# Attention by couples of query rows, with six banks of scores, one bank of turned probabilities and scores five chunks ahead

## The reference, cut to what matters

```
def mla_block_attend(qn, qp, kn, kp, v, qpos, kpos):
    s = jnp.einsum('bqhd,bkhd->bhqk', qn, kn) + jnp.einsum('bqhr,bkr->bhqk', qp, kp)
    s = jnp.where(chunk_mask(qpos, kpos), s.astype(F32) * MLA_SCALE, NEG_INF)
    p = jax.nn.softmax(s, axis=-1).astype(v.dtype)
    return jnp.einsum('bhqk,bkhd->bqhd', p, v)
```

## Time and profile before

| | us |
|---|---|
| median of 3 runs | 3041.34 (3039.64 to 3042.31) |
| the profiled execution | 3039.4 |
| its span, first to last instruction | 3037.6 |
| attention, first S of turn 1 to the end of turn 4 | 1396 to 2058 |
| one turn of chunks (the second), first S to first K of the next | 1566.49 to 1718.61 |

### The profile page before, as it was taken

The page is one execution under the profiler, slowest core; times in us unless marked ns, Lnnn a source line. Parts: engine busy times, 40 slices in busy tenths (PEclk is TensorE's granted clock), DMA queues, the critical chain, the costliest instruction groups (busy, mean ns, idle before and its releaser), DMA issues. The chain is left out here.

```text
span 3037.6 us, 69418 instructions
## 1 busy us (share of the span) xinstructions
PE 2722.8 (90%) x28140; PEld 2005.5 (66%) x28140; DVE 1761.0 (58%) x3745; ACT 1090.9 (36%) x2589; POOL 551.4 (18%) x516
## 2 busy tenths in 40 slices
PE   6999999999999999957989999898998399999970
PEld 6988888888888888844555555554554255555540
DVE  1566666666666666655767586772322644444428
ACT  1233333333333333324545454551222033333336
POOL 0000000000000000001000000001111356566635
PEclk9999999999999999969999999999999699999995
DMA  6222222122221212232010101004554399999537
GB/s 202 40 39 39 39 38 41 37 41 38 40 38 38 38 37 41 41 80 91 1 41 1 41 1 38 1 1 157 156 160 145 152 318 338 370 325 297 135 71 242
DMA packets 336907, 303.11 MB, mean 100 GB/s; under 512 B 236655, under 2 KB 291983, under 8 KB 322193
## 3 DMA queue, kind: packets, MB, share of 16 engines
q1 hardware_dynamic: 318016, 248.31, 26.9%
q0 software_dynamic: 18576, 50.36, 7.1%
HBM read 208.64 MB, written 85.47 MB: 97 GB/s over the span
## 5 line engine op out<-in xcount | busy, mean ns | idle before, releaser
L801 PE MATMUL mx_bank<-mx_xT,mx_w_in 128*128 128x128 f32 x5168 | 646.0, 281 | 18.5 <-DVEq L264 13.7
L801 PEld LDWEIGHTS mx_bank<-mx_xT,mx_w_in 128*128 128x128 f32 x5168 | 600.5, 193 | 62.1 <-issue 37.5
L1502 PE MATMUL at_bank<-pl_kT,pl_qT 128*128 128x512 f32 (+5 forms) x656 | 288.4, 526 | 2.3 <-issue 2.3
L2245 POOL DMA_INDIRECT ex_x<-scr_hx,ex_plan x192 | 239.2, 1246 | 65.2 <-issue 57.9
L1464 ACT ACTIVATE at_PQ<-at_bank,at_nms 128x512 f32<-128x512 f32 (+5 forms) x328 | 193.6, 596 | 118.6 <-DVE at_nms L1603 115.6
L697 ACT ACTIVATE mx_pr<-mx_bank 128x256 f32<-128x256 f32 (+1 forms) x68 | 36.6, 540 | 554.6 <-PE mx_bank L801 471.9
L1534 PEld LDWEIGHTS at_bank<-at_PT,at_vals 128*64 128x64 f32 (+1 forms) x2208 | 117.4, 136 | 146.0 <-issue 81.1
L1599 DVE TENSOR_REDUCE at_mx<-at_bank 128x1 f32<-128x512 f32 (+5 forms) x328 | 188.8, 576 | 43.0 <-PE at_bank L1502 38.5
L652 POOL TENSOR_TENSOR mx_AR<-mx_u,mx_ep 128x512 f32<-128x512 f32 x17 | 20.1, 1181 | 1001.3 <-DVE mx_kh L1141 1001.3
L1514 PE MATMUL at_bank<-pl_at_ident,at_PQ 128*128 128x128 f32 x1104 | 183.6, 281 | 15.9 <-ACT at_PQ L1464 9.8
L1514 PEld LDWEIGHTS at_bank<-pl_at_ident,at_PQ 128*128 128x128 f32 x1104 | 125.7, 140 | 99.3 <-issue 47.7
(11 more groups left out here) (348 smaller groups left out, 5379.3 us busy)
## 6 DMA issues: line engine op xcount, KB each, us to landing
pl_wg<-in_w_eg SPq DMA_DIRECT2D x32, 1024.0 KB, 8.8
pl_wu<-in_w_eu SPq DMA_DIRECT2D x32, 1024.0 KB, 13.0
pl_wd<-in_w_ed SPq DMA_DIRECT2D x32, 1024.0 KB, 9.1
mx_x<-in_x SPq DMA_DIRECT2D x76, 128.0 KB, 3.8
scr_acc<-ro_blank SPq DMA_DIRECT2D x19, 512.0 KB, 6.3
pl_ro_x<-in_x SPq DMA_DIRECT2D x17, 512.0 KB, 5.4
scr_hx<-ro_h SPq DMA_DIRECT2D x17, 512.0 KB, 2.7
scr_acc<-ro_ha SPq DMA_DIRECT2D x17, 512.0 KB, 3.2
```

The costliest lines, as they stand in the source:

```text
L801: ins = pe.matmul(dst, w_in[:, k, col:col + n], xT[:, k, :], start=(k == 0), stop=(k == KC - 1))
L1502: t.mark(pe.matmul(bank[n % SB][:, 0:wd], qT[h][keys(h), j * P:(j + 1) * P], kT[h][keys(h), k0 * P:k0 * P + wd], start=True, stop=True), f ...
L2245: x_in[s].go(g.indirect_dma_start(x[s][:, k, :], None, rows, bass.IndirectOffsetOnAxis(ap=idx[:, at:at + 1], axis=0)))
```

## The change

The rows are taken in couples (0,1), (2,3) to (14,15), and 16 alone. PV of a couple takes one key block for both rows at once where both see it (256 columns), and for the higher row alone where only that one does (128 columns). PT is laid out in 16 slots that hold a chunk of each row of the couple, side by side. The units of a couple start only when the higher row's head 1 chunks are turned, and are given to every second step, two key blocks at a time, or four a step for the couple before the last row. Bank 7 holds 256 columns of sums and 256 of reciprocals, and recT, its copy and out are done once for a couple. AHEAD becomes 5, SB 6 and TB 1. A turn then has 33 steps with units, 74 key blocks (64 of them for two rows, so 138 units as before) and 9 row ends.

```diff
-    AHEAD, SB, TB = 4, 5, 2
+    AHEAD, SB, TB = 5, 6, 1
     LAG = 3
-    NP, NPT = 4, 14
+    NP, NS = 4, 16
...
+    couples = [(j, j + 1) for j in range(0, NT - 1, 2)] + [(NT - 1,)]
...
+    step = 0
+    for q, js in enumerate(couples):
+        mine = [(g, s) for p, g, s in pairs if p == q]
+        following = 2 * len(couples[q + 1]) * len(groups(couples[q + 1][-1])) if q < last_couple else 0
+        stride = 2 if following >= 4 else 1
+        burst = max(2, -(-len(mine) // max(1, following // 2))) if stride == 2 else 4
+        step = max(step, place[js[-1], 1, 0] + LAG)
+        for at in range(0, len(mine), burst):
+            part = mine[at:at + burst]
+            step = max(step, place[js[-1], 1, part[-1][0]] + LAG)
+            share[step] = len(part)
+            last_step = step
+            step += stride
+        row_end[last_step] = q
+        step = max(step, last_step + 2)
...
+                            for h in range(2):
+                                hs = slice(64 * h, 64 * h + 64)
+                                slot = slot_of[place[high, h, gi]] % NS
+                                left = vals[0:rows, k0 + s, hs]
+                                if both:
+                                    ins = pe.matmul(bank[7][hs, 0:2 * P].rearrange("p (a n) -> p a n", a=2), left,
+                                                    PT[0:rows, slot, :, s, :], start=first, stop=end)
...
+                for r in range(len(couples[q])):
+                    ins = pe.transpose(bank[7][:, (2 + r) * P:(3 + r) * P],
+                                       wide[:, q % 2, r].rearrange("p a n -> p (a n)"), ident[:, :])
+                t.mark(ins, f"recT{q}")
...
+                t.mark(v.tensor_tensor(o_sb[:, js[0]:js[-1] + 1, :], bank[7][:, 0:wd].rearrange("p (a n) -> p a n", n=P),
+                                       recb[:, 0:wd].rearrange("p (a n) -> p a n", n=P), ALU.mult), f"out_{j}")
```

More of the change, by code:

```diff
@@ L1279, in ends @@
         return n == count - 1 or chunks[n + 1][:2] != chunks[n][:2]
-    pairs = [(j, g, s) for j in range(NT) for g in range(len(groups(j))) for s in range(groups(j)[g][1])]
-    share, row_end = {}, {}
[L1284 to L1292, removed]
+    couples = [(j, j + 1) for j in range(0, NT - 1, 2)] + [(NT - 1,)]
+    couple_of = {j: q for q, js in enumerate(couples) for j in js}
+    last_couple = len(couples) - 1
+    turned = [(q, h, g) for q, js in enumerate(couples) for h in range(2) for g in range(len(groups(js[-1])))]
+    slot_of = {}
+    for m, (q, h, g) in enumerate(turned):
+        for j in couples[q]:
+            slot_of[place[j, h, g]] = m
+    freed_by = {n: turned[m - NS] for n, m in slot_of.items() if m >= NS and chunks[n][0] == couples[turned[m][0]][0]}
+    pairs = [(q, g, s) for q, js in enumerate(couples) for g in range(len(groups(js[-1]))) for s in range(groups(js[-1])[g][1])]
+    share, row_end = {}, {}
+    step = 0
[13 more added lines that the diff above has]
+        step = max(step, last_step + 2)
     steps = max(max(share) + 1, count)
@@ L1311, in pv_names @@
         out = []
-        for j, g, s in pairs[first:first + share.get(n, 0)]:
-            if s == groups(j)[g][1] - 1:
-                out.append(f"PV{j}_{g}")
+        for q, g, s in pairs[first:first + share.get(n, 0)]:
+            if s == groups(couples[q][-1])[g][1] - 1:
+                out.append(f"PV{q}_{g}")
         return out + ([f"recT{row_end[n]}"] if n in row_end else [])
@@ L1531, in values, with row_rec @@
                             rows = last if s == k - 1 else P
+                            first = gi == 0 and s == 0
+                            both = len(js) == 2 and k0 + s <= low
                             end = gi == len(gs) - 1 and s == k - 1
-                            for h, m in ((0, m0), (1, m1)):
-                                ins = pe.matmul(bank[7][64 * h:64 * h + 64, 0:P], vals[0:rows, k0 + s, 64 * h:64 * h + 64],
-                                                PT[0:rows, m % NPT, s, :], start=(gi == 0 and s == 0), stop=end)
+                            for h in range(2):
[5 more added lines that the diff above has]
+                                                    PT[0:rows, slot, :, s, :], start=first, stop=end)
+                                else:
+                                    c = P * (len(js) - 1)
+                                    ins = pe.matmul(bank[7][hs, c:c + P], left, PT[0:rows, slot, high % 2, s, :],
+                                                    start=first, stop=end)
                             if s == k - 1:
-                                t.mark(ins, f"PV{j}_{gi}")
+                                t.mark(ins, f"PV{q}_{gi}")
                             yield
-            def row_rec(t, j):
-                t.w(vec, f"rec_wide{j}_1")
-                t.mark(pe.transpose(bank[7][:, P:2 * P], wide[:].rearrange("p a n -> p (a n)"), ident[:, :]), f"recT{j}")
+            def row_rec(t, q):
+                t.w(vec, f"rec_wide{couples[q][-1]}_1")
+                for r in range(len(couples[q])):
+                    ins = pe.transpose(bank[7][:, (2 + r) * P:(3 + r) * P],
+                                       wide[:, q % 2, r].rearrange("p a n -> p (a n)"), ident[:, :])
+                t.mark(ins, f"recT{q}")
             def turn(t):
@@ L1639, in turn @@
                         t.w(ten, f"PT{n}")
-                        if n >= NPT:
-                            j, _, g = chunks[n - NPT]
-                            t.w(ten, f"PV{j}_{g}")
+                        if n in freed_by:
+                            q, _, g = freed_by[n]
+                            t.w(ten, f"PV{q}_{g}")
                         wd, _ = width(n)
```

55 lines of the change are left out of this document (31 added, 24 removed).

## The result

The changed kernel takes 3070.76 us in the median of 4 runs (3067.07 to 3072.73), the kernel before 3041.82 in the runs beside it. The ratio is 1.0097, with a 95% interval of 1.0085 to 1.0110: slower by about 29 us, where +14 was forecast. The profiled execution took 3070.69 us, its span is 3068.8, against 3039.4 and 3037.6.

The account below looks back on a forecast made before the run. PE was taken as the bound, 137.4 of 152.1 us a turn. First steps +0.1, middle -0.4 and tail +3.8 made +3.5 a turn, +14 in four, so 3055 us, range 3047 to 3062 (0.43).

Parts of the forecast that it names:

- +1.9 and -2.3: Middle of a turn: steps 24 to 47 become 1.9 us longer, steps 48 to 75 become 2.3 us shorter.
- 256 columns do run side by side: Units of couples: the rival said they don't, so units double, 29 us a turn, 3170; chance 0.02.
- products cost by number: Bursts: rival that half of the 0.33 us goes with product count, 3.5 us a turn, 3041; extreme 3011; chance 0.05.
- The 60 cycles for each matmul: PE's passes, 1184 for 2208: the skill's overhead rule would gain 26 us more than the sum, 3029.
- the sum for a turn: Whole turn: +0.1 first steps, -0.4 middle, +3.8 tail, together +3.5 us, +14 in four turns.
- the clock is no part of this: PE in turn 2 of the kernel before: granted clock of 1.00, so no term for the clock.
- Steps 0 to 23: Start of a turn: one more max, 0.3 us less of outs, bank waits about as large as old waits; +0.1 us.
- Tail, +3.8: From T75 to the next turn: 16.7 us for 12.9, of which 3.2 are the 15 units moved there.
- PE behind a copy, 0.06: T waiting for a copy: PE starts 0.06 us behind the DVE result, part of the 1.49 us T to T.
- a slower edge: Bound T: rival that PE follows a copy by 0.15 us, some 30 T a turn lose 0.09 each, 3066; chance 0.15.
- The bank's wait is covered: Middle of a turn: rival that waits stay below 5.1 us; with 1 us of them, 3025; chance 0.17.
- half the waits: Middle of a turn: rival with 4.3 us of waits, 3038 with the tail's share, up to 3047; chance 0.18.

Follow-up runs that it names:

- e1: The changed kernel with the banks of before: five banks of scores, two of turned probabilities, scores four ahead; 3016.97 us, ratio 0.9926 to the kernel before.
- e11: The kernel before with up to six units in a step in place of three, rows and banks as they were; 3039.79 us, ratio 0.9998.
- e3: The changed kernel with products of latents that nothing reads put into PE's longest waits, at steps 1, 2, 3, 77 and 78; 3057.92 us, ratio 1.0062.
- e7: The changed kernel with DVE's copy of chunk n ahead of the max of chunk n + 5, the row sum and the out; 3051.17 us, ratio 1.0033.
- e8: The changed kernel with two banks of turned probabilities, scores four ahead, and the last three rows alone; 3009.16 us, ratio 0.9894 to the kernel before.
- e9: e8 with two more products a turn that nothing reads, ahead of the last units and at the turn's end; 3007.80 us, ratio 0.9886.
- e12: e9 with three more products that nothing reads, at steps 2, 4 and 5 of a turn; 3008.75 us, ratio 0.9890 to the kernel before.

## Why the prediction was right and wrong

**Right: the direction, and the mechanism in the middle.** The single bank makes T wait for the copy, and with the longer tail this outweighs the PE work saved. From T23 to T75 after takes 95.06 us; with the 85.5 of work that I counted, 9.6 are waits, where I had 8.5. By stretches it is +2.7 and -2.0 against +1.9 and -2.3, so the middle became 0.7 longer and not 0.4 shorter. The count of work holds where a run can show it: in e1 T23 to T47 takes 37.91 us, and I had 37.9. Bursts and units cost what they should:

```profile
1706.46 1.02 PE L1522 MATMUL at_bank<-pl_kT,pl_qT 128*128 128x512 f32 x2
1707.41 1.08 PE L1562 MATMUL at_bank<-at_PT,at_vals 128*64 128x256 f32 x8
1708.43 0.55 PE L1534 MATMUL at_bank<-pl_at_ident,at_PQ 128*128 128x128 f32 x3
```

S to units 0.95, and eight passes of 256 columns, two at a time, in 1.02, as 0.853 and 0.17: so 256 columns do run side by side, and that rival is out. So is *products cost by number*. Its prices were wrong as well: with 0.33 us spread over the twelve products of a burst of three units, after's 296 products a turn would cost 8.1 us for the 10.9 of 33 bursts, a gain of 2.8 at most and of 1.4 by half, not 11 and 3.5. With half the products a burst of the same columns takes the same 1.02 (1620.27 in e11, 1707.41 here). The 60 cycles for each matmul of the Trainium skill (TensorEngine Tiling (Array Packing), Instruction Overhead) are not seen; e1 issues 1024 passes fewer in all, and its 22.7 us fall short of what bursts and recT alone come to (6.7 in each of four turns).

**What failed: the sum for a turn, +3.5 forecast, +7.5 measured in turn 2.** The path was right and its terms were too small, above all because "the clock is no part of this" put the clock at nothing: it cost 2.3 us of the 4.0. The 4.0 are:

- *Steps 0 to 23, "+0.1"*: +1.3. "DVE was the bound and they were free" was wrong in both directions, and hid two large terms: work taken off PE counts there, and so does a later copy. e1 against before shows that the couples save 4.5 us there, and after against e1 that the bank costs 5.8. That the sum of the two came out near my +0.1, but for the clock, was luck. I held new waits on DVE to be about as large as the old ones. I did not walk the first steps, where T1 waits for a copy behind six maxes: 3.0 us at once. e3 puts 0.9 of the +1.2 that I missed down to the clock.
- *The clock, "no part of this"*: 2.3 us a turn (0.9 and 1.4, by e3), more than half of the 4.0. The reading of the earlier trace rows was right for before and said nothing of a kernel with new idle time. Before itself shows the clock down behind the ends of three turns and near the start of one, where PE waits; I should have carried it to the tail that I had made longer by three waits in a row.
- *Tail, +3.8*: +5.5, and 1.4 of the 1.7 is the clock. At full clock e3's tail is 16.96 against 16.7 forecast, so the 15 units and the chain of T76 to T78 (4.52 us, 4.3 forecast) were sized well.
- *PE behind a copy, 0.06*: 0.15 in all the waits of the middle. Over the turns it is 0.14 to 0.15 in 52 of the 78 waits of T and 0.10 in 26; what makes the difference no run shows, but T behind S has no change of tile width, so that isn't needed for 0.15. "No row shows PE released by a copy itself" was a wrong reading: before's T2 at 1572.16, which the profile puts down to exp of a corner, starts 0.11 behind the end of the copy of chunk 0, at 1572.05. With the middle's waits 1.1 larger than forecast, the rival *a slower edge* was the right one in kind. It had put 0.09 on 30 waits a turn, 2.7 us; the middle shows at most 1.1 of that. Its 3066 is nearest to the 3071 measured by luck, as most of what was missed is the clock.

What was missed is 1.2 + 1.7 in the two ends and 0.8 + 0.3 in the middle, 4.0; of the 1.1 in the middle the edge of 0.09 more is the likely cause, not a shown one. *The bank's wait is covered* and *half the waits* fell with the 9.6 us of waits in the middle. That the price of the bank would come out of DVE's order, and could be cut by 20 us with the copy ahead (e7), I had not seen; I had DVE's order in the steps without units only.

**The kernel that beats both** is e8, the couples with two banks and four ahead, the last three rows alone: 3009.2 us, ratio 0.9894 (0.9878 to 0.9911), 2.0% under after. e9 and e12 can't be told from it.

## What to carry to other kernels

When a change gives up a second buffer, write down the round trip through the one that is left (here T, copy, T: 1.41 to 1.50 us for 512 columns) for every kind of step, the first ones too, and compare it with what the waiting engine has to do meanwhile; where the trip is longer, work saved on that engine is worth nothing there. Then look at what the new idle time does to the clock: price the work behind each long wait of TensorE at the lower level. And when one change bundles a gain with a cost, measure the four combinations; here the half that was a gain was hidden behind the half that wasn't.

## What the hardware showed that was not expected

- The granted clock fell from 1.00 to 0.51 and 0.57 behind stretches in which PE was busy 3.22 of 6.70 and 2.15 of 4.49 us, with no single wait over 3.0 us. Products that nothing reads, put into these waits, made the kernel 12.8 us faster (e3). Filling one wait can move the fall to the next one: in e9 it went from the keys to the first steps.
- PE starts 0.10 or 0.15 us behind the end of a DVE copy that it waits for, and 0.14 behind ACT's (78 waits in after). The profile can name another engine, or none, for such a wait; the end of the copy just ahead of it tells.
- At the low clock T of four blocks takes 1.02 us to the units behind it (1720.23 to 1721.25) in place of 0.56 (1715.87 to 1716.43 in e3), and S of 512 columns 1.71 in place of 0.854; engines other than PE keep their times (the max of 512 columns at 1588.66 takes 0.69, as in the earlier trace rows).
